# Inverse roots as a logarithm and an exponential in a two-layer decoder kernel, and a sigmoid from an exponential

## What is computed

```
def rms_norm(x, gain=None):
    y = x * lax.rsqrt(mean(x * x, axis=-1, keepdims=True) + EPS)
    return y * gain if gain is not None else y

h = x + 0.5 * post(swiglu(pre(x)))       # swiglu: (silu(gate) * up) @ w_out, D 1024, FF 2816
h = h + post(token_mixing(pre(h)))       # w_in 1024 x 10248, three branches, gates, w_out
h = h + 0.5 * post(swiglu(pre(h)))

# inside token_mixing, the gated-delta branch
beta = jax.nn.sigmoid(b_raw)                              # the write gate
g = -jnp.exp(a_log) * jax.nn.softplus(a_raw + dt_bias)
q = l2_normalize(q) * DK ** -0.5 ; k = l2_normalize(k)    # also rsqrt(sum + EPS)
o = rms_norm(o, norm_w) ; o = o * silu(z)
```

## Time and profile before

| | us |
|---|---|
| runs | 1865.48, 1869.85, 1864.84 |
| median | 1865.48 |
| span of the profiled execution | 1861.5 |
| TensorE busy in it | 1810.6 |
| VectorE busy | 1344.2 |
| ScalarE busy | 902.9 |
| GpSimd busy | 118.5 |

### The profile page before, as it was taken

One profiled execution on the slowest core, in us unless ns is written; L12 is line 12 of the kernel. 1 busy time (PEld: TensorE's weight loads), 2 busy tenths in 40 slices (PEclk: granted clock), 3 DMA queues, 4 the chain that ended last, 5 costly groups with the idle time before them and its releaser, 6 DMA issues.

```text
span 1861.5 us, 40412 instructions
## 1 busy us (share of the span) xinstructions
PE 1810.6 (97%) x16247; PEld 1746.6 (94%) x16247; DVE 1344.2 (72%) x2096; ACT 902.9 (49%) x1051; POOL 118.5 (6%) x174
## 2 busy tenths in 40 slices
PE   7999999999999999999999999999999899999998
PEld 6999999988989999999999999999889899989998
DVE  6777577787777868877577765868777776887764
ACT  5443354546574254543354434465567545354433
POOL 0000001111210100000000000010112010000000
PEclk9999999999999999999999999999999999999999
DMA  7776666766864656566667766676778465546654
GB/s 231 216 206 192 178 196 221 237 226 216 276 227 139 192 169 220 162 191 168 173 188 212 205 184 198 198 247 201 232 235 283 138 205 170 181 129 189 182 163 133
DMA packets 433619, 368.20 MB, mean 198 GB/s; under 512 B 9395, under 2 KB 411125, under 8 KB 432811
## 3 DMA queue, kind: packets, MB, share of 16 engines
q1 hardware_dynamic: 409560, 276.60, 50.0%
q0 software_dynamic: 23872, 89.03, 14.2%
HBM read 338.90 MB, written 26.69 MB: 196 GB/s over the span
## 4 chain that ended last, share of the span: by engine, by line
PE 71%; DVE 16%; issue 5%; ACT 4%; DMA 2%; DVEq 0%; SPq 0%; ACTq 0%
PE proj L686 46%; PE proj L709 4%; PE proj L704 4%; PE proj L705 4%; DVE wl L1859 3%; ACT wh L1364 2%; PE aux L749 1%; PE proj L660 1%; PE aux L919 1%; PE aux L1141 1%; PE aux L864 1%; PE aux L880 1%; DVE y L2053 1%; DVE x L2054 1%; DMA raw<-w_mem_v 1%
## 5 line engine op out<-in xcount | busy, mean ns | idle before, releaser
L1859 DVE TENSOR_TENSOR wl<-raw,wh 128x2048 fp32r<-128x2048 f32 (+1 forms) x280 | 599.2, 2140 | 193.2 <-ACT wh L1364 167.9
L1364 ACT CAST wh<-raw 128x2048 fp32r<-128x2048 f32 (+1 forms) x280 | 500.3, 1787 | 249.3 <-PE proj L686 105.9
L686 PE MATMUL proj<-xl,wh 128*128 128x264 f32 x2624 | 381.4, 286 | 1.9 <-DVEq L2009 1.3
L686 PE MATMUL proj<-xh,wh 128*128 128x264 f32 x2624 | 380.1, 287 | 0.0
L686 PE MATMUL proj<-xh,wl 128*128 128x264 f32 x2624 | 372.0, 284 | 1.8 <-DVE wl L1859 1.1
L686 PEld LDWEIGHTS proj<-xl,wh 128*128 128x128 f32 x2624 | 341.3, 188 | 15.5 <-issue 13.2
L686 PEld LDWEIGHTS proj<-xh,wl 128*128 128x128 f32 x2624 | 339.0, 188 | 4.2 <-DVE wl L1859 3.9
L686 PEld LDWEIGHTS proj<-xh,wh 128*128 128x128 f32 x2624 | 340.0, 188 | 3.1 <-issue 0.8
L705 PE MATMUL proj<-hl,wh 128*128 128x264 f32 x704 | 173.3, 283 | 0.0
L704 PE MATMUL proj<-hh,wh 128*128 128x264 f32 x704 | 173.0, 283 | 0.0
L1385 ACT ACTIVATE gate<-gate 128x264 f32<-128x264 f32 x88 | 37.4, 425 | 246.2 <-DVEq L1895 246.2
(11 more groups left out here) (477 smaller groups left out, 2271.5 us busy)
## 6 DMA issues: line engine op xcount, KB each, us to landing
raw<-ffn_w_in SPq DMA_DIRECT2D x176, 512.0 KB, 5.1
raw<-w_in SPq DMA_DIRECT2D x80, 1024.0 KB, 5.6
raw<-ffn_w_out SPq DMA_DIRECT2D x64, 704.0 KB, 4.6
sring<-cache_mem_k POOLq DMA_DIRECT2D x32, 512.0 KB, 5.1
sring<-cache_mem_v POOLq DMA_DIRECT2D x32, 512.0 KB, 4.0
out<-sring POOLq DMA_DIRECT2D x32, 512.0 KB, 4.5
sring<-state_gdn POOLq DMA_DIRECT2D x30, 512.0 KB, 5.1
raw<-w_mem_v SPq DMA_DIRECT2D x8, 1024.0 KB, 6.9
```

The lines of the kernel that those rows point to most:

```text
L686: mm = pe.matmul(o, w[:, s, k * 256 + t * P:k * 256 + (t + 1) * P], a[:, k, :], **go)
L1364: act.copy(wh[:, slot, 0:size], raw[:, slot, 0:size]).then_inc(hi_done[slot], 1)
L1859: dve.tensor_sub(wl[:, slot, 0:size], raw[:, slot, 0:size], wh[:, slot, 0:size].bitcast(F32)).then_inc(split_done[slot], 1)
```

## The change

`root()` takes a logarithm into `rt` and then an exponential of -0.5 times it in place, which gives the inverse root itself, and the reciprocals of `rt`, `srs` and `ex` on VectorE are gone. Instead of leaving the choice of table set to the function, the kernel names one set that holds both Ln and Exp ahead of each place where they are used. The Sqrt of one element in `root_table()` becomes this naming alone. The write gate becomes 1 / (1 + exp(min(-b, 80))): on VectorE the sign and the bound ahead of the Exp, the addition and a reciprocal behind it.

```diff
+LOG_EXP = "natural_log_exp_and_others"
             def root(l, name, out, copies=1):
                 o = take(act, l, name)
-                order(act.activation(rt[:], o[:, 0, 0:T], ACT.Sqrt, bias=epst[:], scale=1.0 / (copies * D)))
+                order(act.activation(rt[:], o[:, 0, 0:T], ACT.Ln, bias=epst[:], scale=1.0 / (copies * D)))
                 release(act, name)
+                order(act.activation(rt[:], rt[:], ACT.Exp, scale=-0.5))
                 act.sem_inc(M[out], 1)
             def root_table():
-                order(act.activation(srs[:, 0:1], epst[:], ACT.Sqrt))
+                act.preload_act_table_set(LOG_EXP)
...
             # the same pair for srs and ex, and the table named ahead of it
-                        order(act.activation(gb[:, :, 4:8], gb[:, :, 4:8], ACT.Sigmoid))
+                        order(act.activation(gb[:, :, 4:8], gb[:, :, 4:8], ACT.Exp))
...
             # inverse_root, retention_roots (g 2 and 4), sample_norm, prompt_roots (g 2)
+                    act.preload_act_table_set(LOG_EXP)
...
             # VectorE: the reciprocals of rt at the head of hidden_tile, norm_x and add_result, of srs and ex
-                        order(dve.reciprocal(rt[:], rt[:]))
...
             # VectorE, write gate, ahead of "ab_neg" and behind "ab_exp"
+                        order(ts_(gb[:, :, 4:8], gb[:, :, 4:8], -1.0, 80.0, ALU.mult, ALU.min))
+                        order(ts_(gb[:, :, 4:8], gb[:, :, 4:8], 1.0, None, ALU.add))
+                        order(dve.reciprocal(gb[:, :, 4:8], gb[:, :, 4:8]))
```

More of the change, by code:

```diff
@@ L1352, in _ @@
             order.fresh()
-            order(act.activation(smx[0:32, 0:1], epst[0:32], ACT.Sqrt))
+            act.preload_act_table_set(LOG_EXP)
             act.wait_ge(pro_act, 2)
-            order(act.activation(srs[:], srs[:], ACT.Sqrt, bias=epst[:], scale=1.0 / D))
+            order(act.activation(srs[:], srs[:], ACT.Ln, bias=epst[:], scale=1.0 / D))
+            order(act.activation(srs[:], srs[:], ACT.Exp, scale=-0.5))
             act.sem_inc(pro_act, 1)
@@ L1682, in prepare_delta @@
                         j = g - 2
+                        if g in (2, 4):
+                            act.preload_act_table_set(LOG_EXP)
                         o = take(act, l, f"gn{j}")
@@ L1817, in _ @@
             act.wait_ge(pro_pe, 10)
-            order(act.activation(ex[:, 0:2 + NS], proj[0][:, 0:2 + NS], ACT.Sqrt, bias=epst[:], scale=1.0 / D))
+            order(act.activation(ex[:, 0:2 + NS], proj[0][:, 0:2 + NS], ACT.Ln, bias=epst[:], scale=1.0 / D))
+            order(act.activation(ex[:, 0:2 + NS], ex[:, 0:2 + NS], ACT.Exp, scale=-0.5))
             act.sem_inc(pro_act, 1)
@@ L1850, in _ @@
             dve.wait_ge(pro_act, 3)
-            order(dve.reciprocal(srs[:], srs[:]))
             for t in range(2):
@@ L2668, in _ @@
             dve.wait_ge(pro_act, 6)
-            order(dve.reciprocal(ex[:, 0:2 + NS], ex[:, 0:2 + NS]))
             def add_rows(t, c, bank, turned, kept):
```

## The result

The changed kernel takes 1850.68 us (median of 4 runs, 1849.90 to 1851.62) against 1865.16 for the kernel before: ratio 0.9919, 95% interval 0.9906 to 0.9931. Timed once more beside it, with 5 rounds: 1851.06 (0.9925, 0.9913 to 0.9937). It is faster, as forecast, but by 14.5 us where 10.5 were forecast, and the time lies under the range. The profiled execution has a span of 1848.1, 13.4 under the one of before. In every execution with a span on record the time is 1.8 above the span; the execution whose trace was read before the forecast thus took 1863.3 and was itself 2.2 under its kernel's median. That accounts for about 1 us of the 4; the other 3 are in the sum, and they are what the rest is about.

What follows compares the result with a forecast made beforehand. TensorE, busy 97% of the span, was taken as the bound, so only its idle time and low clock could shrink. Ten places summed to -10.5 us: 1865.5 to 1855.0, own range 1852.5 to 1858, stated range 1852 to 1862.

Steps and rivals of the forecast that it cites:

- 1, p2 of layer 0: Norm p2, layer 0: without the reciprocal on VectorE, TensorE's xh·wl product starts earlier, -1.80 us.
- 2, p3: Norm at the start of layer 1: reciprocal and one-element Sqrt go, the Exp is added, -1.75 us.
- 3, the clock: At p3: with most of TensorE's idle gone, the granted clock no longer falls, -1.5 us, bounds 0 and 1.5.
- 4, p2 of layer 1: Norm p2, layer 1: the root sets the start, and four waits for `xh` pairs shrink, -1.4 us.
- 5, n2: p1 and n2, mk into mq: `wl` starts earlier without the reciprocals, -1.3 us, in layer 1 -0.9.
- 6, start of FFN-in: Four FFN-in starts: Silu's table load becomes exposed; TensorE saves a wait of about 0.3 each, together -1.16 us.
- 9: Additions: six small VectorE instructions in the attention, +0.6 us, bounds 0 and +1.3; new layer 0 table load 0.
- 10: Other table loads that go, in attention, gate, sample softmax and branch roots: 0, bounds 0 and -1.5 us.
- A': Rival: the clock falls all the same, at p3 or another norm, so 1.5 isn't had; 1856.5 us, chance 0.14.
- C: Rival: a table switch costs more than its load, delaying Silu at four FFN starts; 1859.2 us, chance 0.04.
- B: Rival: gains at p2 and p3, 6.45 us, turn into waits for `wh`; 1861.4 us, chance 0.18.
- D: Rival: ScalarE becomes waited for, each of 11 Exps pushing the weight casts, +7.6 us, 1873.1 us; chance 0.04.

Runs made afterwards that it cites:

- the experiment: The changed kernel with a reciprocal on VectorE again at norm p2 of layer 0 alone, behind an Exp of +0.5; span 1851.5 us, +3.4.

## Why the prediction was right or wrong

- *The bound and the price of the new root*: right. Ln 482, Exp 425 ns; the root is paid for only where it sets VectorE's start.
- *1, p2 of layer 0, 1.80*: right; 1.83 by the experiment.
- *2, p3*: over by 0.4, -1.36 for -1.75. The root's price was right, but the weight cast ahead of it now waits 0.37 longer for its transfer, and the root, VectorE and TensorE come later by as much. First before, then after:

```profile
946.68 1.91 ACT L1364 CAST wh<-raw 128x2048 fp32r<-128x2048 f32 x1 [0.35 <-DMA raw<-w_mem_v]
941.28 1.91 ACT L1366 CAST wh<-raw 128x2048 fp32r<-128x2048 f32 x1 [0.72 <-DMA raw<-w_mem_v]
```

- *3, the clock*: right against this trace, -1.54 for -1.5. That p3, the clock and the FFN-in behind them come out as -3.6 for -3.5 is luck: p3 was 0.4 over and the FFN-in (0.7 for 0.27) 0.4 under. The clock is no fixed price either. The trace of before happened to have the fall there; in other executions it is at p2 or at neither, and without it 0.4 to 0.8 was gained, not 1.5.
- *4, p2 of layer 1*: right in sense, -2.05 with its FFN-in start of 0.6 to 0.7, so -1.4 of its own.
- *5, n2*: mis-sized. The forecast took one wait (0.65) and part of others. There are three delayed sets in each layer before, with 0.98 (layer 0) and 0.74 (layer 1) of idle time in the rows, and the rest under the set ahead or in restarts: -1.5 in layer 1 for -0.9, and -1.8 in layer 0 for -1.3, of which about 0.3 isn't the reciprocals'. In layer 0, the set that starts 1.47 behind the one ahead of it where 0.97 is due shows 0.33:

```profile
268.31 1.13 PE L686 MATMUL proj<-xh,wh 128*128 128x264 f32 x8
269.78 1.26 PE L686 MATMUL proj<-xh,wl 128*128 128x264 f32 x8 [0.33 <-DVE wl L1859]
```

- *6, start of FFN-in*: this is the step that failed most. "What this buys TensorE is the wait of about 0.3 for the second `wl`": it bought 0.6 to 0.7 each time, 2.7 for 1.16. I read one wait on the weight load's row. TensorE's own rows show two to three delayed sets, each with a restart of 0.11 to 0.12 in its busy time, and with waits of which they show only 0.11 to 0.13 as idle. Silu behind its exposed table load came 0.65 earlier, as worked out, and that was enough to remove them all.
- *7, gz*: right, -0.59 for -0.55. *8, tail*: right. *9*: the additions cost 0. The +0.6 came out as +0.5 by accident, from small steps of other cause. *10*: right, 0, though the loads that go there are fourteen (sixteen less the two of gz), not twelve.
- *The waits*: the 4.4 for VectorE's low parts was read as standing behind norms. Only 1.3 of it does, and the other 3.1, in the branches, is not the change's to win.
- *The rivals*: A' didn't come about at a norm, though the clock fell in the branches; C didn't: no row has an activation that waits behind its table load. B came about in small: the wait for one transfer took 0.37 of p3's gain and none of the others'. D: ScalarE's slack was real; with 0.55 more the cost is 3.4, not 6.
- *The range*: it was built around the sum with an error of 3 us on its fast side. Prices for n2 and the starts of FFN-in came from idle time, and an error in these has one sign: every wait removed there gave more than its idle time. The 2.9 that the span lies under the sum are 1.6 for FFN-in, 1.1 for n2 and 0.4 for the `wl` at p2, less the 0.4 at p3; the rest is 0.2 in small terms. The 4.0 between span and median was also not a property of the kernel (it is 1.8) but of a fast execution.

## What to carry to other kernels

Price a removed wait of TensorE by the distance of the starts of equal sets of matmuls, not by the idle time in brackets: here the brackets left out up to 0.16 of the wait itself and 0.10 to 0.12 us of restart, both counted as busy. Where a short engine chain feeds several engines (root, scale, Silu, cast, low part), look for all the waits that hang on it; one removed delay ended up to three. Don't compare two totals of busy or of idle time before the granted clock of both traces has been gone through: a fall ahead of a wait moves time from one to the other and costs nothing. And of a single trace take the clock and the branches (layer 1's differed by 0.6 and 0.8 us between two executions of the same program) as one draw, and see that the profiled execution is near the median before it is made the base of the sum.

## What the runs showed of the hardware

- A wait of 0.03 to 0.27 us between matmuls costs TensorE another 0.10 to 0.12 us. With the part of each wait that lies under the set ahead, that is 6.0 us of busy time between the two kernels for the same instructions, the clock's share left out.
- Pauses of 0.2 to 0.6, 1.1 and 0.4 to 0.8 us within 4 us were followed by the 1.2 GHz level for 3 to 4 us in 5 of 10 cases, and the products behind them took 1.5 us longer. With the reciprocal gone and pauses of at most 0.6 left, none of 12 places had it. What a fall costs the kernel depends on what follows: 1.5 at p3 where the FFN-in behind has no reciprocal; where it has one, 0.4 to 0.8 at p3 and 1.3 at p2 of layer 0; nothing in the branches ahead of a wait of 1.6.
- The reciprocal takes 1803 ns for 264 columns where the exponential takes 425: an inverse root as Ln and Exp moves 1.80 us off VectorE for 0.43 on ScalarE.
